# Placing SBUF tiles at multiples of 32 bytes instead of multiples of 128

## What is computed

```
h = h + mixer_ab(rmsnorm(h, g), w_in_ab, ..., w_out_ab)      # 1024x3672, 1024x1024
h = h + square(relu(rmsnorm(h, g) @ w_up[0])) @ w_down[0]     # 1024x4096, 4096x1024
h = h + mixer_c(rmsnorm(h, g), w_in_c, ..., w_out_c)          # 1024x3072, 1024x1024
h = h + square(relu(rmsnorm(h, g) @ w_up[1])) @ w_down[1]
h = concat(meta_tokens, h)                                    # 272 tokens
merged = gate0 * (fourier_mix(u) @ w_fourier) + gate1 * ((b * dwconv(c * v)) @ w_conv_out)
h = h + rmsnorm(merged @ w_out, g)
up = dwconv(rmsnorm(h, g) @ w_up_2)                           # 1024x5632
h = h + rmsnorm((gelu(a) * v) @ w_down_2, g)                  # 2816x1024
```

## Time and profile before

| | |
|---|---|
| time, median of 3 runs | 984.81 us (984.79 to 984.89) |
| the profiled execution: its time | 984.89 us |
| the profiled execution: its span, first to last instruction | 983.1 us |
| granted TensorE clock over the span | 0.998 of full speed |
| HBM read | 166.49 MB |

### The profile page before, as it was taken

The page is one execution under the profiler, slowest core; times in us unless marked ns, Lnnn a source line. Parts: engine busy times, 40 slices in busy tenths (PEclk is TensorE's granted clock), DMA queues, the critical chain, the costliest instruction groups (busy, mean ns, idle before and its releaser), DMA issues.

```text
span 983.1 us, 14080 instructions
## 1 busy us (share of the span) xinstructions
PE 971.7 (99%) x5806; PEld 858.0 (87%) x5806; DVE 611.0 (62%) x894; ACT 553.4 (56%) x832; POOL 130.3 (13%) x44
## 2 busy tenths in 40 slices
PE   9999999999999999999999999999999999999997
PEld 7888888888888788888888888899999999999885
DVE  4997956777312554547777312376547689888643
ACT  6676347666433577846766433544454587665532
POOL 0011041000665000011000666300000000000000
PEclk9999999999999999999999999999999999999999
DMA  8454224555555543335545555464443535555541
GB/s 335 175 178 165 86 86 172 191 195 176 195 186 196 190 167 134 129 133 177 207 171 198 184 178 211 142 215 153 153 166 130 214 118 205 185 198 175 188 155 43
DMA packets 24804, 168.46 MB, mean 171 GB/s; under 512 B 2781, under 2 KB 3092, under 8 KB 4900
## 3 DMA queue, kind: packets, MB, share of 16 engines
q1 hardware_dynamic: 24452, 167.22, 47.2%
q10 hardware_dynamic: 288, 0.33, 0.1%
HBM read 166.49 MB, written 1.05 MB: 170 GB/s over the span
## 4 chain that ended last, share of the span: by engine, by line
PE 95%; ACT 2%; DVE 1%; DMA 1%; issue 0%; SPq 0%; DVEq 0%; ACTq 0%
PE bank L665 23%; PE bank L666 23%; PE bank L667 23%; PE bank L747 12%; PE bank L751 6%; PE bank L883 2%; PE bank L693 1%; DMA raw<-w_stream 1%; ACT whi L1186 1%; DVE wlo L1750 0%; PE bank L851 0%; PE bank L900 0%; PE bank L1094 0%; PE bank L993 0%; PE bank L1078 0%
## 5 line engine op out<-in xcount | busy, mean ns | idle before, releaser
L1750 DVE TENSOR_TENSOR wlo<-raw,whi 128x2048 fp32r<-128x2048 f32 (+2 forms) x152 | 310.7, 2045 | 266.0 <-ACT whi L1186 265.8
L1186 ACT ACTIVATE whi<-raw 128x2048 fp32r<-128x2048 f32 (+1 forms) x154 | 293.0, 1903 | 151.7 <-PE bank L667 148.9
L2422 POOL TENSOR_TENSOR wlo<-raw,whi 128x1024 fp32r<-128x1024 f32 (+1 forms) x37 | 129.1, 3493 | 496.0 <-ACT whi L1186 488.6
L747 PE MATMUL bank<-nhl,whi 128*128 128x512 f32 x512 | 130.4, 395 | 0.0
L667 PE MATMUL bank<-mhi,wlo 128*128 128x258 f32 x384 | 108.9, 284 | 0.0
L665 PE MATMUL bank<-mhi,whi 128*128 128x258 f32 x384 | 108.7, 283 | 0.0
L747 PEld LDWEIGHTS bank<-nhl,whi 128*128 128x128 f32 x512 | 92.2, 189 | 18.7 <-DVE nhl L1758 1.6
L666 PE MATMUL bank<-mlo,whi 128*128 128x258 f32 x384 | 108.3, 282 | 0.0
L665 PE MATMUL bank<-nhl,whi 128*128 128x258 f32 (+3 forms) x320 | 92.9, 290 | 0.0
L666 PE MATMUL bank<-nhl,whi 128*128 128x258 f32 (+3 forms) x320 | 91.3, 285 | 0.0
L667 PE MATMUL bank<-nhl,wlo 128*128 128x258 f32 (+3 forms) x320 | 90.5, 283 | 0.0
(11 more groups left out here) (298 smaller groups left out, 1757.9 us busy)
## 6 DMA issues: line engine op xcount, KB each, us to landing
raw<-w_stream SPq DMA_DIRECT2D x154, 1024.0 KB, 4.8
cst<-consts SPq DMA_DIRECT2D x1, 1200.0 KB, 11.6
h<-x_rows SPq DMA_DIRECT2D x4, 256.0 KB, 5.4
raw<-w_stream SPq DMA_DIRECT2D x2, 512.0 KB, 6.5
out_rows<-e SPq DMA_DIRECT2D x4, 256.0 KB, 2.1
e<-g_post SPq DMA_DIRECT2D x1, 512.0 KB, 3.7
raw<-w_stream SPq DMA_DIRECT2D x1, 352.0 KB, 9.5
b<-consts_x SPq DMA_DIRECT2D x1, 272.0 KB
```

Source lines behind the costliest of these rows:

```text
L747: return pe.matmul(us[c].t[:, :], w[:, k, c * P:c * P + P].hi, nboth[:, k, :], start=k == 0, stop=k == 7)
L1186: act.activation(whi[j][:, 0:n], raw[j][:, 0:n], ACT.Copy).then_inc(s_hi.up(i))
L1750: dve.tensor_tensor(wlo[j][:, 0:m], raw[j][:, 0:m], whi[j][:, 0:m].bitcast(F32), ALU.subtract).then_inc(s_lod.up(i))
L2422: pool.tensor_tensor(wlo[j][:, m:n], raw[j][:, m:n], whi[j][:, m:n].bitcast(F32), ALU.subtract).then_inc(s_lop.up(i))
```

## The change

Sizes and starts are rounded to smaller units. The helper `whole_lines`, which rounds up to 128 bytes, goes. The base is rounded to 64 bytes, and the sizes of tiles to 32. No instruction is added, removed or moved: without the addresses, each engine's list of instructions and waits is the same, only that lines stand 7 lower.

```diff
-LINE = 128
-def whole_lines(n):
-    return -(-n // LINE) * LINE
...
-        base = whole_lines(nc.sbuf_base)
+        base = -(-nc.sbuf_base // 64) * 64
...
-            place[0] += whole_lines(4 * n)
+            place[0] += -(-4 * n // 32) * 32
...
-        place[0] = o_clo + whole_lines(8 * N2 * 4)
+        place[0] = o_clo + -(-8 * N2 * 4 // 32) * 32
...
-                self.at += whole_lines(4 * n)
+                self.at += -(-4 * n // 32) * 32
...
-        o_meta = (end - 4 * (2 * D + 8 * META)) // LINE * LINE
+        o_meta = (end - 4 * (2 * D + 8 * META)) // 32 * 32
```

More of the change, by code:

```diff
@@ L406, in block_kernel @@
     with ctx:
-        base = whole_lines(nc.sbuf_base)
+        base = -(-nc.sbuf_base // 64) * 64
         end = nc.sbuf_usable_end
-        ctx.enter_context(nc.sbuf_tensor("arena", [P, (end - base) // 4 - LINE // 4], F32))
+        ctx.enter_context(nc.sbuf_tensor("arena", [P, (end - base) // 4 - 32], F32))
         place = [base]
```

## The result

The changed kernel takes **991.48 us** (median of 4 runs, 991.35 to 991.60), the kernel before 984.84 us in the same comparison (984.79 to 984.89): ratio 1.0066, 95% interval 1.0054 to 1.0079. It is 6.6 us slower, 1 us above the upper end of the forecast range, and on the side and in the place of rival A.

What follows compares the result with a forecast made beforehand. PE was taken as the bound, busy 971.7 of 983.1 us. Profiled 984.89 us plus 0.5 (term 3), all other terms 0, gave 985.4, as a median 985.3 us; own range 984.0 to 987.2, 8-in-10 range 983.3 to 990.5.

Steps and rivals of the forecast that it cites:

- rival A: All three down projections slow to the output projections' pace: +4.1 us, 990 us in all (989 to 992); chance 0.23.
- What bounds the kernel: Whole kernel: time is the number of matmuls times PE's starting pace, plus about 11 us in which PE waits.
- what does not move: raw, whi, wlo, h, nhl, chi, mhi, thus the weight chain and matmuls in proj, mlp and on nhl: cost 0.
- Term 1: Down projections, 1032 matmuls with f, g, e stationary and now off multiples of 128: 0 taken, upper end +4.1 us.
- Term 2: Output projections, 192 matmuls, clo moved by 64 against chi: 0 taken, bounds -0.8 and +0.8 us.
- Term 3: 258-column matmuls, 1152 of them, mlo moved by 64 against mhi: +0.5 us, bounds 0 and +1.
- Term 4: Plain float32 matmuls of areas a, c, b, some 680 records: 0, up to 2.7 us if term 1 reached its upper end.
- Term 5: DVE, ACT and POOL operations on tiles now at 32, 64 or 96 modulo 128: 0 taken, bound +0.5 us.
- Term 6: Other transfers, cst landing at 64 modulo 128 and four outputs: 0 taken, bounds -0.1 and +0.3 us.
- The rule weighed: PE's two independent read ports: addresses of f, g, e could not matter, 985.3 us; not followed, because of 4 ns unexplained.
- B: Faster: output projections fall to 227 ns (-0.8 us) and 258-column stages gain (-1.3 us), 982.7 us; chance 0.09.
- C: Slower by a transfer: cst over 5 us longer or last output twice as long, +2 to +4 us; chance 0.06.

Runs made afterwards that it cites:

- the map: Separate kernel, only PE working, stationary tile at varied distances from the moving tile; with 512 columns 227 ns at 256 bytes, 233 at 16, 32 and 384.
- e3: Kernel before with only the low half of each pair moved, f by 128, g by 64, e by 32 bytes: 990.30 us (one run).
- e4: Kernel before with its base 32 bytes further, so every tile but the three meta tiles moves and distances stay: 984.67 us, ratio 0.9999.
- e6: Kernel before with nhl alone 64 bytes further and all tiles behind it 256 further: 984.98 us (one run).
- e8: Kernel before repacked, 512-column stages' tiles multiples of 256 apart, wlo 64 bytes further in its slot for 32 tiles: 983.21 us, ratio 0.9982.
- e10: As e8, but wlo 8 bytes further in its slot instead of 64 for the same 32 tiles: 982.85 us, ratio 0.9979 to the kernel before.
- e7: Kernel before with clo 128 bytes further and everything behind it 256 further: 983.97 us, ratio 0.9992.
- two maps: The map and its repeat for 256, 258 and 272 columns, stationary tiles 1024 instead of 2048 bytes apart; at distance 96, 256 columns: 120 and 117 ns.

## Why the prediction was wrong

**What bounds the kernel** was right: PE's pace sets the end, and the effect is one of pace. So was what does not move: the stages on `nhl` kept 227.7 ns.

**Term 1**, the pace of the down projections, is the step that failed, twice. I put its lower end, 0, at the `KEYS` matmuls, and took it. Their stationary pieces are off the grid, but only 256 columns move there. The map shows that with 256 columns a displaced tile costs nothing (118 ns for 120), and with 512 columns 6 ns. The row was nearest in the offset and far in the shape, and the shape decided. I also put the missing 2 ns down to the narrower load. The map has them at full width: over the eight distances that the pieces of `KEYS` take (0, 32, 64 and so on to 224) its mean is 118.2 ns, the 118 of the row. So they can be the effect itself, with the other sign; no run tests 88 columns alone. Then the upper end, +4.1 us: the output projection's 231 ns was read as the price of a displaced tile. It is a mean over triples of which only the low half is displaced; e3 shows the one at 227 and two at 233 to 234. Had I read the starts of a triple one by one I would have had 6 to 7 ns, and 1032 x 6.5 = 6.7 us. It came out at 6.5 us.

**The variable** was wrong as well. I compared high half with low half (128 apart modulo 1024) and absolute offsets with multiples of 128. `clo` starts on a multiple of 128 and is slow, which spoke against the second reading in the very row I used. Had I listed each fast and slow stage's distance between stationary and moving tile modulo 256 (0 in `f`, `g`, `e` and `nhl`, 128 in `clo`), the pattern was there before the change was run: `f` and `g` go to 224, `e` to 160.

**Term 2** right: 231.3 to 231.0 ns, -0.1 us. `clo` goes from 128 to 64; both are slow. **Term 3** right in being small: 668 for 669, and +0.3 us over the 1152 matmuls by the sum of the starts; the matmuls on `FT` and `YB` gave back 0.2. **Term 4** right: paces in `a` and `c` are the same to 1 ns, where moving and stationary tile come from one area or 128 columns move (why those with another distance don't change was not tested); that the 2.7 us would follow term 1 was not so. **Term 5** right:

```profile
L2353 DVE SCALAR_TENSOR_TENSOR e<-bank,vec,e 128x255 f32<-128x255 f32 x40 | 19.3, 483 | 1.4
L2350 DVE SCALAR_TENSOR_TENSOR e<-bank,vec,e 128x256 f32<-128x256 f32 x40 | 19.1, 478 | 0.0
```

These are the groups of the earlier trace rows after the change, at 483 and 478 ns as before. The aligned form now reads at 32 modulo 128 and costs nothing more; that 4 bytes further on is the worst offset, as I wrote, no run tests. **Term 6** right: the transfers of the earlier trace rows after; `cst` lands at 16.5 us as before, and PE first uses it at 21.7.

```profile
cst<-consts SPq DMA_DIRECT2D x1, 1200.0 KB, 11.3
out_rows<-e SPq DMA_DIRECT2D x4, 256.0 KB, 2.1
```

**Two numbers** of the prediction are off and change nothing here. The ends of terms 2, 3, 5 and 6 add up to 983.9 to 987.4 us, not 984.0 to 987.2. And the 156 weight tiles hold 162.9 MB, not 166; 166.49 MB is all that was read.

**The rule weighed.** By the two independent read ports of the Trainium skill (SBUF — State Buffer, Who interferes with whom) term 1's upper end was 0. The measurement decides against that reading: e4, e6 and the map show that PE's pace depends on the distance between what it reads as moving and as stationary operand, by 7 ns in the map (226.7 to 234.0) with nothing else running, and by up to 12 ns for one position of a triple in e3 (226.8 to 238.9).

**The rivals.** A was the case, with its place right (all three down projections) and its price of 4.1 us too small by more than a third of the 6.5; its own range, 989 to 992, held the result. I gave it 0.23 since `KEYS` seemed to speak against it. The range ended at 990.5, inside A, and so missed by 1 us. B did not come about by this change; that the present places are not the best was true (e8 and e10; e7's interval includes no change). C did not occur.

## What to carry to other kernels

When a change moves only addresses, list for each kind of matmul the distance from stationary to moving tile, and compare stages by it; a tile's own offset said nothing here (e4). For long moving operands (512 columns) keep the two a multiple of 256 bytes apart, which costs a few hundred bytes of padding and here is worth 6.5 us of 985; for short ones another distance can be a little better, and must be measured in the kernel's own sequence. A row used as a bound has to match in the shape that sets the pace, not only in the property that changes.

## What was not expected of the hardware

A stationary tile off by 8 to 224 bytes (modulo 256) slows a matmul with 512 moving columns from 226.7 ns to between 229 and 234, with 384 columns by 0 to 3 ns, and with 256 columns it leaves it at 120 or speeds it up, to as little as 113.4. The load's own duration does not change (188 to 189 ns on PEld for every tile of the first map but `d0x`, which began with the slow starts). Distance 240 behaves as 0 at 512 columns, and 16 does not. Paces in a mixed sequence are not the sum of the map's values: 113.4 ns alone was 117.7 between 512-column matmuls. The period of 256 bytes rests on 512 columns (256, 512 and 1024 at 227 ns, 384 as 128); with 256 columns two maps gave different paces at 96, 128 and 240. What inside PE or its memory reads makes the period was not found, and no run here tests it.
